# Linear attention levels with 64-row products: one query operation for both heads, results by head

## The chip, the cores and the metric

One core of a Trainium2 chip runs the whole program in one launch. The metric is device time in microseconds (us) of one execution, median of three. The engines are TensorE (PE), VectorE (DVE), ScalarE (ACT), GpSimd (POOL) and the DMA queues that SyncE (SP) starts.

## The reference, cut to what matters

The program is a two-layer block (pooling, gated linear attention, softmax attention, MLP) followed by a second block (Mamba-2, gated delta rule, MLP). The change touches the gated linear attention alone, 4 heads of 64, over 256 context and 512 latent tokens:

```python
def gla_chunk_scan(q, k, v, la, s0, strict):
    mask = np.tril(np.ones((C, C), bool), k=-1 if strict else 0)[:, :, None]
    def step(S, inp):
        qc, kc, vc, lc = inp
        b = jnp.cumsum(lc, axis=2)
        o_inter = jnp.einsum('bhid,bhde->bhie', qc * jnp.exp(b), S)
        diff = b[:, :, :, None, :] - b[:, :, None, :, :]
        decay = jnp.exp(jnp.where(mask, diff, -jnp.inf))
        A = jnp.einsum('bhid,bhjd,bhijd->bhij', qc, kc, decay)
        o = o_inter + jnp.einsum('bhij,bhje->bhie', A, vc)
```

It runs forward (f) and backward (b) in time. The decay is per channel d, so A is no plain product of queries and keys.

## The kernel before, in words

The function `gla` computes this in tiles of 128 tokens. It is called twice: for layer 0 (all C = 6 tiles, `first` = 0, nb = 6) and for layer 1 (the 4 latent tiles, `first` = 2, nb = 4). For stable exponents it splits each 128x128 matrix A into **levels**: at level m (1, 2, 4, ... 64) the queries are the second halves of blocks of 2m tokens and the keys the first halves, and both are scaled against the decay at the middle. 7 levels forward and 7 backward make 14 levels a layer. Only half of the tokens are queries in a level, so a tile has 64 query columns.

A level goes through four engines, each with its own written-out order and semaphores:

- POOL, lines 1142 to 1155: 4 subtractions give the exponents in `E` (two buffers, by `lev % 2`); it may begin level lev once `level_ready` of lev - 2 is up, then it raises `diff`.
- ACT, line 1106: one Exp over `E`, raises `ee`.
- DVE, `decayed(lev)`, lines 1206 to 1221: one product for the keys into `F` (L1216) and two products of 64 partitions each for the queries into `Q` (L1220), then `level_ready`. A partition group of 64 is one head of a pair. `Q` is zero outside: head 0's queries have data in partitions 0 to 63 and zeros below, head 1's the reverse; a MEMSET (L1162) sets the zeros at the start of the stage.
- PE, L1039: for each tile and pair of heads one fp32 product over all 128 rows, whose 128 moving columns are 64 queries of head 0 and 64 of head 1. The zeros keep the heads apart. 4 products fill a bank of PSUM and raise `a_full`; banks go round by 6, and PE waits for `a_read` before it fills one again. An fp32 product is two LDWEIGHTS and two MATMUL records in the trace.
- DVE, L1238: a COPY_PREDICATED per bank (512 columns) puts the wanted entries into `A`, raises `a_read`.

DVE's order is: `decayed(lev + 1)`, then the copies of level lev, and so on, so PE works on level lev + 1 while DVE copies level lev:

```python
                for lev in range(1, 2 * LEVELS + 1):
                    if lev < 2 * LEVELS:
                        decayed(lev + 1)
                    ...
                    for n in range(nb // 2):
                        done = (lev - 1) * (nb // 2) + n
                        dve.wait_ge(a_full, done + 2)
```

After the 14 levels ACT waits for the last `a_full`, and writes the state decays into the same memory `qd` that held `Q` (L1113); DVE multiplies them (L1244), and chunk states, output products (L1067, L1070) and the gate follow. Ahead of the levels the own-token products L1025 contract over 64 rows each: its banks alternate between partitions 0 to 63 and 64 to 127. The stage loads nothing large and has a barrier at both ends. PE also runs the pool mix (L1006) after levels 3 and 6, ACT its results (L1085).

## Time and profile before

| | |
|---|---|
| three runs | 4133.22, 4142.72, 4141.39 us, median 4141.39 |
| the profiled execution | 4152.68 us, span 4149.8 us |
| PE busy over the span | 3610.2 us, 87% |
| DVE busy | 2273.7 us, 55% |
| ACT, POOL busy | 1255.5 us, 30%; 1162.5 us, 28% |
| mean granted TensorE clock | 0.916 |
| levels of layer 0 | about 314.5 to 400 us of the span |
| levels of layer 1 | about 1560.5 to 1618 us |

Times are us from the span's start. PE is the matmul, PEld the weight load beside it; L12 is line 12. In a row of the timeline several alike instructions in a row are merged: start, how long they took together, engine, line, operation, tiles, count, and in brackets the idle time before and who ended it. A granted clock of 1.00 is 2.4 GHz, 0.50 is 1.2 GHz.

### The profile page before, as it was taken

The numbers are of one execution on the slowest core, as the hardware profiler recorded it, in microseconds if no ns is written. First come the engines' busy times: TensorE is split into PE (matmuls) and PEld (weight loads), VectorE is DVE, ScalarE is ACT, GpSimd is POOL, SyncE is SP. The second block draws the span as 40 slices with busy tenths as digits, with TensorE's granted clock in tenths as the row PEclk, the third lists the DMA queues.
The fourth block names the chain that finished last, engine by engine and source line by source line (L and its number), as shares of the span: only waits on it lengthen the run. The fifth ranks groups of instructions, "written<-read, shape, count | busy, mean of one in ns | idle before, by whom it ended". The sixth has DMA issues, their size and how long they took to land. (4 is left out here: it accounts for less than half of the span.)

```text
span 4149.8 us, 56879 instructions
## 1 busy us (share of the span) xinstructions
PE 3610.2 (87%) x22004; PEld 3014.9 (73%) x22004; DVE 2273.7 (55%) x3284; ACT 1255.5 (30%) x1878; POOL 1162.5 (28%) x564
## 2 busy tenths in 40 slices
PE   5976797899998976889996999798999996987998
PEld 3766576788887765667885788677777775765886
DVE  4669462655546448535445588733666655326334
ACT  4123222211222123223323354432333432323222
POOL 5214002222222203024441333143222220423442
PEclk8988599899999988999998999899999997998998
DMA  4420001223222430013331211121011110212221
GB/s 164 154 93 1 0 1 61 77 97 112 97 91 93 142 105 1 1 58 115 117 111 44 77 66 71 36 102 67 32 47 37 41 47 1 102 61 72 98 95 60
DMA packets 85332, 295.30 MB, mean 71 GB/s; under 512 B 13506, under 2 KB 14082, under 8 KB 84740
## 3 DMA queue, kind: packets, MB, share of 16 engines
q1 hardware_dynamic: 84836, 290.74, 19.8%
q8 instruction: 154, 2.52, 0.2%
q10 hardware_dynamic: 288, 1.60, 0.1%
q14 instruction: 54, 0.44, 0.0%
HBM read 290.21 MB, written 2.10 MB: 70 GB/s over the span
## 5 line engine op out<-in xcount | busy, mean ns | idle before, releaser
L221 POOL TENSOR_TENSOR mlp_slab_lo<-slab,mlp_slab_hi 128x1024 fp32r<-128x1024 f32 x192 | 477.1, 2488 | 889.2 <-ACT mlp_slab_hi L204 889.2
L119 PE MATMUL banks<-mlp_hid_hi,mlp_slab_hi 128*128 128x512 f32 (+1 forms) x1024 | 375.0, 366 | 8.9 <-DVE mlp_hid_lo L1798 8.9
L120 PE MATMUL banks<-mlp_hid_lo,mlp_slab_hi 128*128 128x512 f32 (+1 forms) x1024 | 372.7, 364 | 0.0
L121 PE MATMUL banks<-mlp_hid_hi,mlp_slab_lo 128*128 128x512 f32 (+1 forms) x1024 | 372.4, 364 | 0.0
L204 ACT ACTIVATE mlp_slab_hi<-slab 128x1024 fp32r<-128x1024 f32 x192 | 202.4, 1058 | 528.8 <-PE banks L121 400.9
L119 PE MATMUL banks<-hT_mlp_hi,mlp_slab_hi 128*128 128x512 f32 (+1 forms) x768 | 276.6, 360 | 15.5 <-issue 8.7
L1798 DVE TENSOR_TENSOR mlp_hid_lo<-mlp_sq,mlp_hid_hi 128x512 fp32r<-128x512 f32 (+1 forms) x96 | 216.4, 2254 | 117.9 <-ACT mlp_hid_hi L1756 117.5
L120 PE MATMUL banks<-hT_mlp_lo,mlp_slab_hi 128*128 128x512 f32 (+1 forms) x768 | 275.7, 359 | 0.0
L121 PE MATMUL banks<-hT_mlp_hi,mlp_slab_lo 128*128 128x512 f32 (+1 forms) x768 | 274.9, 358 | 0.0
L119 PEld LDWEIGHTS banks<-mlp_hid_hi,mlp_slab_hi 128*128 128x128 f32 x1024 | 194.2, 190 | 43.8 <-DVE mlp_hid_lo L1798 13.8
L121 PEld LDWEIGHTS banks<-mlp_hid_hi,mlp_slab_lo 128*128 128x128 f32 x1024 | 194.0, 189 | 30.3
L120 PEld LDWEIGHTS banks<-mlp_hid_lo,mlp_slab_hi 128*128 128x128 f32 x1024 | 194.1, 190 | 29.6
L221 POOL TENSOR_TENSOR ssm_slab_lo<-slab,ssm_slab_hi 128x1024 fp32r<-128x1024 f32 x48 | 124.0, 2591 | 303.2 <-ACT ssm_slab_hi L204 303.1
L221 POOL TENSOR_TENSOR out_slab_lo<-slab,out_slab_hi 128x1024 fp32r<-128x1024 f32 x24 | 58.9, 2466 | 520.5 <-ACT out_slab_hi L204 520.5
L1795 DVE TENSOR_TENSOR mlp_sq<-mlp_tmp 128x512 f32<-128x512 f32 (+1 forms) x96 | 96.8, 1008 | 196.5 <-ACT mlp_tmp L1751 196.5
L221 POOL TENSOR_TENSOR gdn_slab_lo<-slab,gdn_slab_hi 128x1024 fp32r<-128x1024 f32 x48 | 116.2, 2424 | 283.1 <-ACT gdn_slab_hi L204 283.1
L406 DVE SCALAR_TENSOR_TENSOR mlp_vec_acc<-mlp_vec_slab,c_act,mlp_vec_acc 128x512 f32<-128x512 f32 x192 | 187.6, 1032 | 4.5 <-DMA mlp_vec_slab<-in_s_vec_mlp_dram 4.5
L119 PEld LDWEIGHTS banks<-hT_mlp_hi,mlp_slab_hi 128*128 128x128 f32 x768 | 147.8, 192 | 39.2 <-issue 13.2
L1751 ACT ACTIVATE mlp_tmp<-banks 128x512 f32<-128x512 f32 (+1 forms) x96 | 64.3, 670 | 357.9 <-PE banks L121 347.8
L121 PEld LDWEIGHTS banks<-hT_mlp_hi,mlp_slab_lo 128*128 128x128 f32 x768 | 147.4, 192 | 21.3
L120 PEld LDWEIGHTS banks<-hT_mlp_lo,mlp_slab_hi 128*128 128x128 f32 x768 | 147.7, 192 | 20.6
L221 POOL TENSOR_TENSOR proj_slab_lo<-slab,proj_slab_hi 128x1024 fp32r<-128x1024 f32 x32 | 80.4, 2519 | 262.6 <-ACT proj_slab_hi L204 262.6
(532 smaller groups left out, 9330.4 us busy)
## 6 DMA issues: line engine op xcount, KB each, us to landing
slab<-in_s_mlp_dram SPq DMA_DIRECT2D x192, 512.0 KB, 3.5
proj_vec_slab<-in_s_vec_proj_dram SPq DMA_DIRECT2D x64, 512.0 KB, 3.7
mlp_vec_slab<-in_s_vec_mlp_dram SPq DMA_DIRECT2D x64, 512.0 KB, 3.5
slab<-in_s_ssm_dram SPq DMA_DIRECT2D x48, 512.0 KB, 3.5
slab<-in_s_gdn_dram SPq DMA_DIRECT2D x48, 512.0 KB, 3.5
slab<-in_s_in_dram SPq DMA_DIRECT2D x32, 512.0 KB, 4.6
slab<-in_s_out_dram SPq DMA_DIRECT2D x24, 512.0 KB, 4.2
slab<-in_s_merge_ssm_dram SPq DMA_DIRECT2D x24, 512.0 KB, 3.5
```

The costliest lines, as they stand in the source:

```text
L119: nc.tensor.matmul(out, lhs.hi, rhs.hi, start=start, stop=False)
L120: nc.tensor.matmul(out, lhs.hi, rhs.lo, start=False, stop=False)
L121: return nc.tensor.matmul(out, lhs.lo, rhs.hi, start=False, stop=stop)
L204: self.nc.scalar.activation(hi, self.raw[s][:], ACT.Copy).then_inc(self.rounded, 1)
L221: self.nc.gpsimd.tensor_tensor(pair.lo[:], self.raw[u % slots][:], pair.hi[:].bitcast(F32), ALU.subtract).then_inc(self.split, 1)
L406: last = nc.vector.scalar_tensor_tensor(out=acc, in0=x, scalar=w, in1=acc, op0=ALU.mult, op1=ALU.add)
L1751: nc.scalar.activation(tmp[:, u % 2, :], source(u), ACT.Relu).then_inc(rel, 1)
L1795: nc.vector.tensor_tensor(sq[:, u % 2, :], tmp[:, u % 2, :], tmp[:, u % 2, :], ALU.mult).then_inc(squared, 1)
L1798: nc.vector.tensor_tensor(hid.lo[:, u, :], sq[:, u % 2, :], hid.hi[:, u, :].bitcast(F32), ALU.subtract).then_inc(hid_ready, 1)
```

## The change

- `Q` is now [128, 2, 2, tile, 64]: no half for each head, no zeros. One DVE operation over 128 partitions makes the queries of both heads of a pair. The MEMSET of `qd` goes, and `cleared` is awaited at 3, not 4.
- PE computes each head apart: rows 0 to 63 of `F` and `Q` for head 0, rows 64 to 127 for head 1, one straight after the other, 64 moving columns each. That is twice as many products with half the columns.
- Results are laid out by head: a **part** is up to 4 tiles (layer 0: parts of 4 and 2 tiles, M = 2; layer 1: one part of 4, M = 1) and fills two banks, one for each head. `a_full` is raised once for a part. PE waits until both banks are read.
- DVE copies one bank of a part for each head: 512 columns for a part of 4 tiles, 256 for one of 2.

```diff
+    parts = [(t, min(4, C - t)) for t in range(first, C, 4)]
+    M = len(parts)
...
-        Q = qd[:].rearrange("p d n -> p (d n)").rearrange("p (b h a t f) -> p b h a t f", b=2, h=2, a=2, f=64)
+        Q = qd[:, 0:2, :].rearrange("p d n -> p (d n)").rearrange("p (b a t f) -> p b a t f", b=2, a=2, f=64)
...
+        def filled(lev, j, h):
+            return 2 * ((lev - 1) * M + j) + h
...
-                    for n in range(nb // 2):
-                        done = (lev - 1) * (nb // 2) + n
-                        if done >= 6:
-                            pe.wait_ge(a_read, done - 4)
-                        for e in range(4):
-                            ch = first + 2 * n + e // 2
-                            last = nc.tensor.matmul(c.ps[:, done % 6, e * P:(e + 1) * P].rearrange("p (h f) -> p h f", h=2),
-                                                    F[:, lev % 2, e % 2, ch * P:(ch + 1) * P], Q[:, lev % 2, :, e % 2, ch, :], start=True, stop=True)
+                    for j, (t0, count) in enumerate(parts):
+                        if filled(lev, j, 1) >= 6:
+                            pe.wait_ge(a_read, filled(lev, j, 1) - 4)
+                        for e in range(2 * count):
+                            ch = t0 + e // 2
+                            for h in range(2):
+                                r = slice(64 * h, 64 * h + 64)
+                                last = nc.tensor.matmul(c.ps[:, filled(lev, j, h) % 6, e * 64:(e + 1) * 64], F[r, lev % 2, e % 2, ch * P:(ch + 1) * P],
+                                                        Q[r, lev % 2, e % 2, ch, :], start=True, stop=True)
                         last.then_inc(a_full, 1)
...
-                nc.vector.memset(qd[:], 0.0).then_inc(cleared, 1)
...
-                        dve.wait_ge(a_full, (lev - 2) * (nb // 2) + 1)
+                        dve.wait_ge(a_full, (lev - 2) * M + 1)
                     nc.vector.tensor_tensor(F_[:, :, :, keys], k_[:, :, :, keys], E_[:, :, :, keys], ALU.mult)
-                    for h in range(2):
-                        r = slice(64 * h, 64 * h + 64)
-                        to = Q[r, lev % 2, h, :, first:, :].rearrange("p a t f -> p a (t f)").rearrange("p a (b m) -> p a b m", m=m)
-                        last = nc.vector.tensor_tensor(to, q_[r, :, :, queries], E_[r, :, :, queries], ALU.mult)
-                    last.then_inc(level_ready, 1)
+                    to = Q[:, lev % 2, :, first:, :].rearrange("p a t f -> p a (t f)").rearrange("p a (b m) -> p a b m", m=m)
+                    nc.vector.tensor_tensor(to, q_[:, :, :, queries], E_[:, :, :, queries], ALU.mult).then_inc(level_ready, 1)
...
-                    for n in range(nb // 2):
-                        done = (lev - 1) * (nb // 2) + n
-                        dve.wait_ge(a_full, done + 2)
...
-                        nc.vector.copy_predicated(second(A[:, first + 2 * n:first + 2 * n + 2].rearrange("p t a h f -> p (t a h) f")),
-                                                  mask.to_broadcast([P, 8, 64 // m, m]),
-                                                  c.ps[:, done % 6, :].rearrange("p (e b m) -> p e b m", e=8, m=m)).then_inc(a_read, 1)
+                    for j, (t0, count) in enumerate(parts):
+                        dve.wait_ge(a_full, (lev - 1) * M + j + 2)
+                        for h in range(2):
+                            n = filled(lev, j, h)
+                            if lev > 1:
+                                dve.wait_ge(a_read, n - 2 * M + 2)
+                            nc.vector.copy_predicated(second(A[:, t0:t0 + count, :, h].rearrange("p t a f -> p (t a) f")),
+                                                      mask.to_broadcast([P, 2 * count, 64 // m, m]),
+                                                      c.ps[:, n % 6, 0:128 * count].rearrange("p (e b m) -> p e b m", e=2 * count, m=m)).then_inc(a_read, 1)
```

How DVE's order reads in layer 0 before, from the keys of level 5 on (L1216 the keys, L1220 the queries, L1238 the copies):

```order
L1216 TENSOR_TENSOR gla_r<-gqk,gla_r 128x48x16
L1220 TENSOR_TENSOR gla_qd<-gqk,gla_r 64x768 x2
L1238 COPY_PREDICATED gla_A<-const,banks 128x64x8 x3
L1216 TENSOR_TENSOR gla_r<-gqk,gla_r 128x24x32
L1220 TENSOR_TENSOR gla_qd<-gqk,gla_r 64x768 x2
L1238 COPY_PREDICATED gla_A<-const,banks 128x32x16 x3
```

And with the change, at the same place:

```order
L1222 TENSOR_TENSOR gla_r<-gqk,gla_r 128x48x16
L1224 TENSOR_TENSOR gla_qd<-gqk,gla_r 128x768
L1242 COPY_PREDICATED gla_A<-const,banks 128x8x8x8 x2
L1242 COPY_PREDICATED gla_A<-const,banks 128x4x8x8 x2
L1222 TENSOR_TENSOR gla_r<-gqk,gla_r 128x24x32
L1224 TENSOR_TENSOR gla_qd<-gqk,gla_r 128x768
L1242 COPY_PREDICATED gla_A<-const,banks 128x8x4x16 x2
L1242 COPY_PREDICATED gla_A<-const,banks 128x4x4x16 x2
```

One of two query operations is gone from each level, and three copies have become four, two of them of half size. On PE, the level products of layer 0 before (36 are three levels of 12, L1006 is the pool mix):

```order
L1039 MATMUL banks<-gla_qd,gla_r 128x128 x36
L1006 MATMUL banks<-gla_m,gla_wp 128x512
L1006 MATMUL banks<-gla_m,gla_wp 128x256
L1039 MATMUL banks<-gla_qd,gla_r 128x128 x36
```

and with the change:

```order
L1046 MATMUL banks<-gla_qd,gla_r 128x64 x72
L1012 MATMUL banks<-gla_m,gla_wp 128x512
L1012 MATMUL banks<-gla_m,gla_wp 128x256
L1046 MATMUL banks<-gla_qd,gla_r 128x64 x72
```

Nothing has moved between them; each product of 128 columns has become two of 64.

## Rows read from the trace of the kernel before

**Rows 1.** The page, busy time of engines over the span.
```profile
PE 3610.2 (87%) x22004; PEld 3014.9 (73%) x22004; DVE 2273.7 (55%) x3284; ACT 1255.5 (30%) x1878; POOL 1162.5 (28%) x564
```
**Rows 2.** Busy time by window, levels of layer 0 and of layer 1; PEclk is the clock.
```profile
core 0: us, PE busy (x) PEld busy (x) DVE busy (x) ACT busy (x) POOL busy (x), PEclk, DMA share, GB/s
314.50:400.00 85.50, 55.10 (x344) 51.37 (x344) 82.77 (x86) 25.04 (x23) 47.42 (x48) 0.84 0.00 1
1560.50:1618.00 57.50, 38.24 (x249) 34.19 (x244) 56.12 (x71) 17.02 (x20) 34.88 (x48) 0.85 0.00 1
```
**Rows 3.** Timeline of one level of layer 0.
```profile
341.04 1.90 DVE L1238 COPY_PREDICATED gla_A<-const,banks 128x512 f32<-128x512 uint32 x3
...
341.06 4.58 PE L1039 MATMUL banks<-gla_qd,gla_r 128*128 128x128 f32 x24 [2.36 <-DVE gla_qd L1220]
341.08 0.83 POOL L1150 TENSOR_TENSOR gla_r<-gla_bT 128x384 f32<-128x384 f32 x1 [1.86 <-DVE gla_qd L1220]
...
342.84 1.47 DVE L1216 TENSOR_TENSOR gla_r<-gqk,gla_r 128x768 f32<-128x768 f32 x1
343.45 1.55 POOL L1151 TENSOR_TENSOR gla_r<-gla_bT 128x384 f32<-128x384 f32 x1
344.23 2.55 DVE L1220 TENSOR_TENSOR gla_qd<-gqk,gla_r 64x768 f32<-64x768 f32 x2
345.04 1.49 ACT L1106 ACTIVATE gla_r<-gla_r 128x1536 f32<-128x1536 f32 x1 [4.29 <-POOL gla_r L1151]
346.81 1.95 DVE L1238 COPY_PREDICATED gla_A<-const,banks 128x512 f32<-128x512 uint32 x3
```
**Rows 4.** Timeline of one level of layer 1.
```profile
1583.33 1.32 DVE L1238 COPY_PREDICATED gla_A<-const,banks 128x512 f32<-128x512 uint32 x2
...
1583.36 3.78 PE L1039 MATMUL banks<-gla_qd,gla_r 128*128 128x128 f32 x16 [1.62 <-DVE gla_qd L1220]
...
1585.61 1.79 DVE L1220 TENSOR_TENSOR gla_qd<-gqk,gla_r 64x512 f32<-64x512 f32 x2
1586.19 1.06 ACT L1106 ACTIVATE gla_r<-gla_r 128x1024 f32<-128x1024 f32 x1 [3.04 <-POOL gla_r L1154]
...
1587.43 0.73 DVE L1238 COPY_PREDICATED gla_A<-const,banks 128x512 f32<-128x512 uint32 x1
```
**Rows 5.** Line L1220 by itself, layers 0 and 1: ns min/median/max.
```profile
L1220 DVE TENSOR_TENSOR gla_qd<-gqk,gla_r x28: 923/956/1661, 315.4 to 392.1; 64x768 f32<-64x768 f32 x28
L1220 DVE TENSOR_TENSOR gla_qd<-gqk,gla_r x28: 673/690/1214, 1561.1 to 1614.9; 64x512 f32<-64x512 f32 x28
```
**Rows 6.** Line L1216, the keys, 128 partitions, layer 0.
```profile
L1216 DVE TENSOR_TENSOR gla_r<-gqk,gla_r x14: 947/1400/1747, 314.6 to 390.3; 128x768 f32<-128x768 f32 x14
```
**Rows 7.** Timeline, first levels of layer 0, then of layer 1.
```profile
318.26 3.25 DVE L1220 TENSOR_TENSOR gla_qd<-gqk,gla_r 64x768 f32<-64x768 f32 x2
...
321.55 3.63 DVE L1238 COPY_PREDICATED gla_A<-const,banks 128x512 f32<-128x512 uint32 x3
...
1563.12 0.69 DVE L1216 TENSOR_TENSOR gla_r<-gqk,gla_r 128x512 f32<-128x512 f32 x1 [0.62 <-ACT gla_r L1106]
```
**Rows 8.** Timeline, PE: a full-clock level; 64 columns; 64 rows; 64 by 64.
```profile
335.86 2.84 PE L1039 MATMUL banks<-gla_qd,gla_r 128*128 128x128 f32 x24
...
2356.02 3.68 PE L2052 MATMUL banks<-ssm_xdt,ssm_dec 128*128 128x64 f32 x32
...
1553.72 2.82 PE L1025 MATMUL banks<-gqk 64*128 64x128 f32 x32 [0.69 <-ACT gla_bT L1102]
...
2916.81 1.15 PE L2283 MATMUL banks<-gdn_own,gdn_am 64*64 64x64 f32 x32
```
**Rows 9.** Busy time by window, around the products of L2052.
```profile
2356.00:2380.00 24.00, 22.96 (x162) 21.37 (x161) 17.61 (x32) 9.06 (x17) 6.92 (x3) 1.00 0.12 45
```
**Rows 10.** Timeline, end of the levels of layer 1.
```profile
1615.64 2.05 PE L1039 MATMUL banks<-gla_qd,gla_r 128*128 128x128 f32 x16 [1.17 <-DVE gla_qd L1220]
1617.73 2.77 ACT L1113 ACTIVATE gla_qd<-gla_bT 128x3072 f32<-128x3072 f32 x1 [5.52 <-PE banks L1039]
```
**Rows 11.** Timeline, DVE at the start of the stage in layer 0.
```profile
267.07 2.62 DVE L1162 MEMSET gla_qd<- 128x3072 f32 x1 [0.59 <-issue]
...
283.25 0.53 DVE L1181 RECIPROCAL gla_qk_stat<-gla_qk_stat 128x60 f32<-128x60 f32 x1 [9.50 <-ACT gla_qk_stat L1094]
```

More of the change, by code:

```diff
@@ L1043, in _ @@
                         pool_mix(lev // 3 - 1)
-                pe.wait_ge(a_read, LEVELS * nb + 1)
+                pe.wait_ge(a_read, 4 * LEVELS * M + 1)
                 for t in range(C):
@@ L1110, in _ @@
                         pool_out(lev // 3 - 1)
-                act.wait_ge(a_full, LEVELS * nb + 1)
+                act.wait_ge(a_full, 2 * LEVELS * M + 1)
                 nc.scalar.activation(qd[:], bT[:], ACT.Exp).then_inc(decays, 1)
@@ L1214, in decayed @@
                     if lev > 2:
-                        dve.wait_ge(a_full, (lev - 2) * (nb // 2) + 1)
+                        dve.wait_ge(a_full, (lev - 2) * M + 1)
                     nc.vector.tensor_tensor(F_[:, :, :, keys], k_[:, :, :, keys], E_[:, :, :, keys], ALU.mult)
-                    for h in range(2):
-                        r = slice(64 * h, 64 * h + 64)
-                        to = Q[r, lev % 2, h, :, first:, :].rearrange("p a t f -> p a (t f)").rearrange("p a (b m) -> p a b m", m=m)
-                        last = nc.vector.tensor_tensor(to, q_[r, :, :, queries], E_[r, :, :, queries], ALU.mult)
-                    last.then_inc(level_ready, 1)
-                dve.wait_ge(cleared, 4)
+                    to = Q[:, lev % 2, :, first:, :].rearrange("p a t f -> p a (t f)").rearrange("p a (b m) -> p a b m", m=m)
+                    nc.vector.tensor_tensor(to, q_[:, :, :, queries], E_[:, :, :, queries], ALU.mult).then_inc(level_ready, 1)
+                dve.wait_ge(cleared, 3)
                 decayed(1)
@@ L1231, in _ @@
                     mask = second((c.mask_f if d == 0 else c.mask_b)[:, (lev - 1) % LEVELS:(lev - 1) % LEVELS + 1, :]).bitcast(U32)
-                    for n in range(nb // 2):
-                        done = (lev - 1) * (nb // 2) + n
-                        dve.wait_ge(a_full, done + 2)
-                        if lev > 1:
-                            dve.wait_ge(a_read, done - nb // 2 + 2)
-                        nc.vector.copy_predicated(second(A[:, first + 2 * n:first + 2 * n + 2].rearrange("p t a h f -> p (t a h) f")),
-                                                  mask.to_broadcast([P, 8, 64 // m, m]),
-                                                  c.ps[:, done % 6, :].rearrange("p (e b m) -> p e b m", e=8, m=m)).then_inc(a_read, 1)
-                dve.wait_ge(a_read, LEVELS * nb + 1)
+                    for j, (t0, count) in enumerate(parts):
[7 more added lines that the diff above has]
+                                                      c.ps[:, n % 6, 0:128 * count].rearrange("p (e b m) -> p e b m", e=2 * count, m=m)).then_inc(a_read, 1)
+                dve.wait_ge(a_read, 4 * LEVELS * M + 1)
                 dve.wait_ge(decays, 2)
```

## The prediction

> **What bounds the kernel now.** I read the page first. TensorE is busy for 87% of the span [rows 1], so one would look there. But the change touches only the level loops, two stretches of 85.5 and 57.5 us, and there the busy times by window say something else: VectorE is busy for 82.77 of 85.50 us and 56.12 of 57.50 us, TensorE for 55.10 and 38.24 [rows 2]. Then I read the timeline of one level. In layer 0 VectorE goes without a gap from three copies (341.04) to the keys (342.84), the two query operations (344.23) and the next copies (346.81): a level takes 5.77 us, all of it VectorE [rows 3]. TensorE stood idle for 2.36 us before its products, and the reason named is the query operation L1220. In layer 1 the same loop is 1583.33 to 1587.43, 4.10 us [rows 4]. So VectorE sets the pace of 28 levels, and what it sheds shortens the stage, as long as POOL, ACT and TensorE keep up. The stages behind have barriers between them and start earlier by as much.
>
> **The query operations.** Alone, one takes 0.956 us on 768 columns and 0.690 us on 512, over 64 partitions [rows 5]. What does one over 128 partitions cost? The keys are such an operation with the same 768 columns, and their shortest is 0.947 us [rows 6], so VectorE's time follows the columns and not the partitions. The merged operation costs what one of the two did. Which one goes? The pair takes 2.58 us from start to start of the next (344.23 to 346.81), more than 2 x 0.956, because the first runs beside POOL's last subtraction, which itself takes 1.55 us in place of 0.83 [rows 3]. With a gap of 0.03 us the second takes 0.99, the first 1.59. POOL's work stays, so its cost to VectorE stays, and the free one is what goes: 0.99 us a level in layer 0. In the second level both are stretched (318.26 to 321.55, 3.29 us [rows 7]), and 3.29 - 1.59 = 1.70 go. Layer 0: 13 x 0.99 + 1.70 = 14.5 us. In layer 1 it is 0.69 + 0.03 = 0.72 a level. In its first level nothing is won, since the next keys wait 0.62 us for ACT there already [rows 7]. Layer 1: 13 x 0.72 = 9.4 us.
>
> **The copies.** In layer 0 three copies of 512 columns (1.80 us, 0.60 each [rows 3]) become two of 512 and two of 256. From 768 to 512 columns a query operation loses 0.266 us [rows 5], so 256 columns cost 0.27 us, and a half copy 0.60 - 0.27 = 0.33. Together 1.86 to 1.87, 0.07 more a level, 1.0 us over 14. In layer 1 there are two copies of 512 before and after. The copies of the finest levels are slower (three in 321.55 to some 325 [rows 7]) and stay so, as they touch the same entries. The destination is now cut in more pieces for one instruction. No row shows that alone; the copies of different levels in [rows 3] and [rows 4] have different pieces at the same 0.60, so I take nothing, and 0.1 us a copy (84 copies, 8 us) as the far bound.
>
> **The MEMSET.** It takes 2.62 us, but VectorE then idles 9.50 us until ACT gives the roots [rows 11]. Nothing is won, in either layer. If that cover were gone it would be 2 x 2.6.
>
> **TensorE.** A product before is two records of 128 columns; a level of layer 0 has 24 of them and takes 2.84 us at full clock [rows 8], 4.58 us where the clock changes in between [rows 3]; 16 in layer 1 take 2.05 us at full clock [rows 10] and 3.78 us at low clock [rows 4]. After, there are 48 and 32, with 64 moving columns. Half the columns do not make them faster: 32 records of 128 rows with 64 moving columns take 3.68 us, (3.68 - 0.28) / 31 = 0.110 us each, the spacing of the 128-column ones ((2.84 - 0.28) / 23 = 0.111) [rows 8]. So one record costs a weight load of 128 columns. All hangs on whether the two row halves work at the same time. Two rows say so. The own products use halves of the rows in turns of 8 records and take 2.82 us for 32, 0.082 each, less than a lone load allows. The delta-rule products alternate between row halves at every product, as the change will, and need 1.15 us for 32, 0.030 each, though their loads have 64 columns, which by halving 0.110 would be 0.055 alone [rows 8]. They pair fully. I take full pairing: 48 records in 24 slots of 0.11, the same 2.84 us a level as before, 16 slots in layer 1. The far bound is no pairing, 0.110 a record.
>
> Does TensorE then come in time? VectorE's new level is 5.77 - 0.99 + 0.07 = 4.85 us. Copying now waits for a part of 16 slots (2.05 us, at low clock 3.78), where it waited for one bank; DVE comes for it 4.85 us after `level_ready`. Enough. The part of two tiles waits for the bank pair that DVE reads 1.2 us after `level_ready`, while the first part is still running, so nothing is lost. In layer 1 the new level is 3.38 us, and the single part at low clock is ready after 3.78: a wait of 0.4. The granted clock there is 0.85 over the loop [rows 2], so about 30% of 14 levels, 4 levels or so, wait, and it costs at most 1.7 us; I take 1.0. After the last level ACT waits for TensorE's last result: 1615.64 to 1617.73 [rows 10], the same slots as now.
>
> **POOL and ACT.** From `level_ready` to the end of ACT's Exp two levels ahead it is 341.04 to 346.53, 5.49 us [rows 3]; the keys that need it come 4.85 + 1.87 = 6.72 us after. In layer 1 it is 1583.33 to 1587.25, 3.92 [rows 4], against 3.38 + 1.22 = 4.60. They have 1.2 and 0.7 us to spare.
>
> **The sum**: 14.5 + 9.4 - 1.0 - 1.0 = 21.9 us. Against the profiled execution 4152.7 gives 4130.8 us. That execution lies 11.3 us above the median of the three; against the median, 4141.4 - 21.9 = 4119.5 us. The three runs spread over 9.5 us, 0.23%, so about 0.3% (12.4 us) is what a measurement can tell from no change. My bound for faster is 4129.0.
>
> **Rivals.**
> *Row halves do not pair in full, at full clock.* At 0.110 a record TensorE needs 5.3 us a level in layer 0 and 3.5 in layer 1 and becomes the bound. The gain is 14 x 0.49 + 13 x 0.58 = 14.4 us, less what the last level adds to the way to ACT (24 and 16 slots of 0.11, 4.4 us): 4131.4, no change. A row speaks for full clock: where TensorE is busy for 22.96 of 24 us with products that include the 64-column ones, it is granted 1.00 [rows 9]. The pairing rows speak against it. The Trainium skill, "TensorE: Matmul & The Clock Gate", section on LDWEIGHTS, gives a rule that speaks for this rival: a weight load takes a time set by its columns and not by its rows, so a load of 64 rows is no cheaper, and the loads are doubled here; by that alone TensorE's time would double. The Trainium skill, "TensorEngine Tiling (Array Packing)", section Key Properties, has the counter-rule, that different tiles load and multiply in parallel; the trace agrees with it (0.082 and 0.030 us against 0.110 [rows 8]).
> *Slower: no pairing, and the clock as granted now.* With 0.84 and 0.85 [rows 2] a record costs 0.131 us; a level of layer 0 is 6.29 us on TensorE against 5.77 now, of layer 1 4.19 against 4.10. That is 7.3 + 1.2 us, and 5.2 on the way to ACT behind the last levels: 4155 us. It decides as soon as records come further apart than 5.77 / 48 = 0.120 us in layer 0. Held at low clock (15 spacings in 3.36 us, 0.224 a record [rows 4]) it would be 10.8 and 7.2 us a level, above 4240.
> *Pairing holds, but the clock is lower than now.* Each half of the rows now streams columns half the time. If all levels ran at low clock, layer 0 would take 24 x 0.224 = 5.4 us a level and layer 1 3.8: gains of 5 and 4 us, and 4 lost behind the last levels, some 4136. More low levels than now, but not all, gives 4124 to 4132.
> *The merged operation costs double*, VectorE being charged by partition: then 4142. [Rows 6] speak against it.
>
> **How the numbers follow.** The forecast has 0.70 (its own range 4110 to 4127, from the runs' spread and 0.1 us a copy); pairing with a lower clock, or pairing in part only, 0.14, about half of it on either side of 4129; no pairing at full clock 0.05; slower 0.07; other causes of no change 0.04. Faster 0.77, same 0.16, slower 0.07. The range of 4108 to 4133 us leaves out the slower cases and the far ends.
>
> **What would show it.** In the profile after: query operations x14 a layer at medians near those of the keys, 1.4 to 1.6 us in layer 0; levels of about 4.85 and 3.4 us from first copy to first copy; half copies near 0.33 us apart; level products of 48 records in about 2.9 us at full clock; the loops at 71 and 48 us. Wrong would be: VectorE waiting for PE before copies in most levels, records 0.11 us apart without partners, VectorE waiting for ACT before the keys, or a granted clock in the loops well under 0.84.

## The result: 4105.3 us, 36 us faster, with a lower clock in the loops than forecast

The changed kernel takes 4105.26 us (median of 8 runs, 4088.94 to 4121.81), the kernel before 4141.16 us in the runs beside it (8 runs, 4133.22 to 4152.71): ratio 0.9913, 95% interval 0.9888 to 0.9939. Faster was forecast, at 4119.5 us in a range from 4108 to 4133. The gain came out at 36 us in place of 22, and the time 3 us below the lower end of the range. The profiled execution took 4095.27 us, its span is 4093.5 us.

The page of the kernel after, busy time and instruction queue:

```profile
PE 3608.2 (88%) x22564; PEld 3025.4 (74%) x22564; DVE 2231.0 (55%) x3268; ACT 1253.4 (31%) x1878; POOL 1159.5 (28%) x564
...
q8 instruction: 141, 2.31, 0.2%
```

Against [rows 1] VectorE shed 42.7 us, and TensorE got 560 records more with no more busy time. The busy times of the two level loops, from the first keys to the first product with the decays, answer to [rows 2]:

```profile
core 0: us, PE busy (x) PEld busy (x) DVE busy (x) ACT busy (x) POOL busy (x), PEclk, DMA share, GB/s
308.90:386.30 77.40, 70.22 (x680) 65.82 (x680) 63.63 (x86) 24.38 (x20) 44.42 (x48) 0.59 0.01 1
1505.50:1563.70 58.20, 51.70 (x461) 47.08 (x459) 42.95 (x58) 19.23 (x21) 32.90 (x48) 0.57 0.01 1
```

The same two stretches of the kernel before, between the same two instructions (the windows of [rows 2] begin and end elsewhere):

```profile
314.60:399.00 84.40, 55.10 (x344) 51.37 (x344) 81.67 (x86) 23.94 (x19) 47.42 (x48) 0.84 0.00 1
1560.50:1620.60 60.10, 38.24 (x249) 34.19 (x244) 56.59 (x72) 19.62 (x21) 34.88 (x48) 0.86 0.00 1
```

So the loops gave 7.0 and 1.9 us, 9 in all. VectorE's work fell by more than forecast, 18.0 us (81.67 to 63.63) and 13.6 (56.59 to 42.95) for 13.5 and 9.4. But the granted clock fell from 0.84 and 0.86 to 0.59 and 0.57, TensorE is busy for 70.22 of 77.40 us where it was for 55.10 of 84.40, and where VectorE waits for it, in six of layer 0's 14 levels and ten of layer 1's, it sets the pace now. What VectorE waited for is told by the lines of the stretch 308 to 388 us, layer 0's loop:

```profile
line engine op names shapes xcount | busy us, mean ns | idle before us <-releasers
L1242 DVE COPY_PREDICATED gla_A<-const,banks 128x512 f32<-128x512 uint32 x28 | 22.9, 884 | 9.2 <-PE banks L1046 9.2
...
L1224 DVE TENSOR_TENSOR gla_qd<-gqk,gla_r 128x768 f32<-128x768 f32 x14 | 16.4, 1172 | 0.0
...
L1242 DVE COPY_PREDICATED gla_A<-const,banks 128x256 f32<-128x256 uint32 x28 | 13.0, 529 | 1.9 <-PE banks L1046 1.9
```

The copies waited 9.2 + 1.9 = 11.1 us for TensorE; in layer 1's loop it is 13.1.

L1046 holds the level products now, L1242 the copies, L1224 the queries, L1222 the keys. In the timeline a level at low clock stands like this (its counterpart is [rows 3]):

```profile
start us, us, engine line op out<-in xcount [idle before <-releaser]
336.74 1.32 DVE L1242 COPY_PREDICATED gla_A<-const,banks 128x512 f32<-128x512 uint32 x2 [0.93 <-PE banks L1046]
...
338.44 0.77 DVE L1242 COPY_PREDICATED gla_A<-const,banks 128x256 f32<-128x256 uint32 x2 [0.39 <-PE banks L1046]
...
339.11 0.95 DVE L1222 TENSOR_TENSOR gla_r<-gqk,gla_r 128x768 f32<-128x768 f32 x1
339.98 0.95 DVE L1224 TENSOR_TENSOR gla_qd<-gqk,gla_r 128x768 f32<-128x768 f32 x1
...
341.86 1.36 DVE L1242 COPY_PREDICATED gla_A<-const,banks 128x512 f32<-128x512 uint32 x2 [0.92 <-PE banks L1046]
```

From copies to copies it is 5.12 us (336.74 to 341.86), of which VectorE waits 0.93 + 0.39 for TensorE. The keys and the queries take 0.95 us each here and not some 1.5: while VectorE waits, POOL's subtractions get done, so that its operations no longer run beside them. That is why its busy time fell by more than forecast. Where TensorE's results are there in time, later in the same loop, a level is what was forecast: 367.30 - 362.47 = 4.83 us, without a wait.

```profile
362.47 1.94 DVE L1242 COPY_PREDICATED gla_A<-const,banks 128x512 f32<-128x512 uint32 x4
...
364.32 1.55 DVE L1222 TENSOR_TENSOR gla_r<-gqk,gla_r 128x768 f32<-128x768 f32 x1
...
365.80 1.57 DVE L1224 TENSOR_TENSOR gla_qd<-gqk,gla_r 128x768 f32<-128x768 f32 x1
...
367.30 1.96 DVE L1242 COPY_PREDICATED gla_A<-const,banks 128x512 f32<-128x512 uint32 x4
```

TensorE's own rows show that the halves of the rows pair at either clock: at full clock 32 records take 2.00 us, 16 slots with (2.00 - 0.28) / 15 = 0.115 us between them; at low clock, granted 0.50, TensorE is busy without a break and does 101 records in 11 us, 0.218 for two. The first two rows are the timeline's, the last is the busy time by window.

```profile
352.29 2.00 PE L1046 MATMUL banks<-gla_qd,gla_r 64*128 64x64 f32 x32 [0.25 <-DVE gla_qd L1224]
...
357.44 25.90 PE L1046 MATMUL banks<-gla_qd,gla_r 64*128 64x64 f32 x240 [1.68 <-DVE gla_qd L1224]
...
333.00:344.00 11.00, 11.00 (x101) 10.82 (x100) 8.10 (x14) 2.97 (x2) 6.64 (x9) 0.50 0.01 1
```

So where do 36 us come from, when the loops give 9? I cut both traces at the barriers between stages. The busy times by window of five stages before (linear attention, attention and multilayer perceptron of layer 0, linear attention and attention of layer 1):

```profile
265.49:448.34 182.85, 113.64 (x724) 102.12 (x724) 148.32 (x190) 65.81 (x86) 55.60 (x56) 0.77 0.04 11
451.85:628.40 176.55, 171.74 (x868) 124.83 (x868) 97.76 (x244) 47.50 (x109) 0.00 (x0) 0.82 0.00 1
716.83:1319.82 602.99, 573.31 (x3280) 505.18 (x3280) 343.44 (x376) 131.99 (x162) 166.43 (x64) 0.96 0.27 98
1513.74:1663.73 149.99, 91.58 (x572) 79.98 (x572) 118.75 (x174) 58.76 (x84) 40.84 (x56) 0.76 0.04 13
1667.53:1797.48 129.95, 124.14 (x740) 93.51 (x740) 76.37 (x164) 38.36 (x77) 0.00 (x0) 0.95 0.00 1
```

and the same five after:

```profile
259.71:435.90 176.19, 129.92 (x1060) 117.69 (x1060) 127.79 (x189) 65.92 (x86) 52.37 (x56) 0.65 0.04 12
439.41:589.57 150.16, 145.34 (x868) 107.97 (x868) 95.33 (x244) 47.43 (x109) 0.00 (x0) 0.98 0.00 1
679.34:1265.67 586.33, 567.94 (x3280) 501.65 (x3280) 343.65 (x376) 131.80 (x162) 167.87 (x64) 0.97 0.28 101
1458.76:1607.02 148.26, 104.81 (x796) 92.64 (x796) 102.62 (x159) 58.73 (x84) 39.55 (x56) 0.65 0.04 14
1610.83:1740.88 130.05, 124.30 (x740) 93.71 (x740) 76.39 (x164) 38.33 (x77) 0.00 (x0) 0.95 0.00 1
```

The two stages that the edit changes gave 6.7 and 1.7 us. Layer 0's attention, whose instructions did not change (868 records of TensorE in both), went from 176.55 to 150.16 us with the granted clock from 0.82 to 0.98, and the perceptron behind it, with the same 3280 records, from 602.99 to 586.33. These two give 43.1 of the 56.3 us between the two spans; the projection ahead of the change, which the edit does not touch either and which takes 187 to 192 us in profiles of either kernel, gives 5 more. Between the medians it is less, since the profiled execution of before lies 11.5 us above its median and that of after 10.0 us below.

### The profile page after: what moved, and what is told of

The parts are those of the page before. It is cut to its first block and busy times, and to the rows that moved or that the text cites. A ratio compares the mean times of both kernels' runs of the same rounds, so it can differ in the third digit from the quotient of the medians.

```text
span 4093.5 us, 57957 instructions
## 1 busy us (share of the span) xinstructions
PE 3608.2 (88%) x22564; PEld 3025.4 (74%) x22564; DVE 2231.0 (55%) x3268; ACT 1253.4 (31%) x1878; POOL 1159.5 (28%) x564
## 5 line engine op out<-in xcount | busy, mean ns | idle before, releaser
L119 PEld LDWEIGHTS banks<-mlp_hid_hi,mlp_slab_hi 128*128 128x128 f32 x1024 | 194.4, 190 | 43.3 <-DVE mlp_hid_lo L1802 13.5
```

The source lines that it names most:

```text
L119: nc.tensor.matmul(out, lhs.hi, rhs.hi, start=start, stop=False)
```

## The experiments

My theory for the loops: the clock fell because TensorE streams 64 columns in a slot where it streamed 128, though the slots take the same time. Its rival: the clock fell because VectorE's faster levels bring the products closer together or at other moments. For the two foreign stages the question was whether they vary from run to run, or with something that the change moves.

**Products that stream their columns twice.** The kernel with the change, every product (but the last of a part) over its 64 columns twice in a row; the second copy falls on the entry that the next product writes, so the results are the same.

```diff
-last = nc.tensor.matmul(c.ps[:, filled(lev, j, h) % 6, e * 64:(e + 1) * 64], F[...], Q[r, lev % 2, e % 2, ch, :], ...)
+w = 2 if e < 2 * count - 1 else 1
+last = nc.tensor.matmul(c.ps[:, filled(lev, j, h) % 6, e * 64:(e + w) * 64].rearrange("p (w f) -> p w f", w=w), F[...],
+                        Q[r, lev % 2, e % 2, ch, :].unsqueeze(1).to_broadcast([64, w, 64]), ...)
```

> The changed kernel, but each level product streams its 64 query columns twice (128 moving columns; the second copy lands in the bank's next 64 columns and is overwritten by the next product). Same weight loads, same slots of 0.11 us, same results. Theory 1, the granted clock in the level loops fell from 0.84 to 0.59 because each record streams only 64 columns: now the clock is back at 0.8 or more, VectorE no longer waits 24 us for TensorE before its copies (under 8 us), and the two loops, first keys to the first product with the decays, take about 71 and 50 us in place of 77.4 and 58.2. Theory 2, the clock fell for another reason (row halves used in turns, or shorter levels): clock near 0.6, waits near 24 us, loops 77 and 58. Attention of layer 0: 150 us if it is the levels' ending that decides how it begins, whatever the columns.

Measured: 4105.25 us (8 runs, 4098.41 to 4109.23), ratio to before 0.9933 (0.9912 to 0.9954). Busy time of the two loops by window:

```profile
314.90:385.70 70.80, 50.13 (x680) 46.45 (x680) 67.64 (x85) 23.98 (x19) 48.06 (x48) 0.90 0.01 2
1528.20:1578.90 50.70, 35.55 (x461) 32.07 (x459) 45.44 (x58) 19.06 (x21) 35.41 (x48) 0.90 0.01 2
```

With the same 680 records the clock is back at 0.90, TensorE is busy for 50.13 us in place of 70.22, and the loops take 70.8 and 50.7 us: twice the columns, and 14 us less. The copies wait 0.9 us for TensorE in layer 0 and 2.4 in layer 1, in place of 11.1 and 13.1. One level of layer 0 in the timeline:

```profile
336.14 1.96 DVE L1243 COPY_PREDICATED gla_A<-const,banks 128x512 f32<-128x512 uint32 x4
336.28 2.90 PE L1047 MATMUL banks<-gla_qd,gla_r 64*128 64x128 f32 x48 [1.95 <-DVE gla_qd L1225]
...
340.96 2.00 DVE L1243 COPY_PREDICATED gla_A<-const,banks 128x512 f32<-128x512 uint32 x4
```

48 records in 2.90 us, the slots of [rows 8], and 4.82 us a level. That the whole kernel was no faster than the change lies in layer 0's attention: it takes 171.7 us here, in place of 150.2, so the 150 of the expectation did not come, though the levels end as in the change.

**Both kernels looked at once more.** Neither is edited.

> The kernel before, unchanged, profiled again. In the two profiles attention of layer 0 took 176.6 us before and 150.2 after, the MLP of layer 0 603.0 and 586.4, the projection of layer 0 192.3 and 187.2. Theory A, these belong to the kernels: here again 177 and 603. Theory B, they differ from execution to execution: attention anywhere from 150 to 180, MLP anywhere from 586 to 603.

> The changed kernel, unchanged, profiled again. Theory A: attention of layer 0 again 150 us, MLP again 586, clock in the levels again near 0.59, loops 77.4 and 58.2. Theory B: attention and MLP take other values, up to 177 and 603.

Measured, one run each: before 4137.28 us, its attention 171.8 and its perceptron 597.9 us; the change 4108.4 us, 150.3 and 586.6 us. The loops of before are again 84.4 and 60.2 us, those of the change 79.0 and 59.6. Neither kernel repeats its durations exactly (attention of before was 176.6, its perceptron 603.0), but the two foreign stages are part of the difference in both pairs.

**Half of the query work alone.** The kernel before with head 0's queries only; it leaves out head 1's decayed queries, so head 1's half of the columns holds the zeros of the MEMSET.

```diff
-                    for h in range(2):
+                    for h in range(1):
```

> The kernel before, with VectorE making the queries of head 0 alone in each level (head 1's product is left out, its half of the operand stays zero); TensorE does the 128-column products over 128 rows as before. It has the VectorE side of the change without its TensorE side. Theory 1 (64 columns lower the clock): VectorE sheds 0.99 and 0.72 us a level, the clock stays near 0.84, and the loops take 84.4 - 14 = 70 and 60.1 - 10 = 50 us. Theory 2 (shorter levels lower the clock): clock under 0.7 and loops of 75 and 56 or more.

Measured: 4121.14 us (10 runs, 4098.2 to 4129.61), ratio 0.9954 (0.9930 to 0.9978), loops of 74.0 and 52.4 us. VectorE makes one query operation a level here, as in the change, and TensorE still streams 128 columns a record. The two loops by window:

```profile
310.60:384.60 74.00, 49.30 (x344) 45.98 (x344) 69.62 (x71) 23.95 (x20) 57.58 (x48) 0.91 0.00 1
1539.80:1592.20 52.40, 33.84 (x249) 29.45 (x244) 45.62 (x57) 19.31 (x21) 41.23 (x48) 0.97 0.00 1
```

The clock is 0.91 and 0.97. Shorter levels do not lower it; the rival falls. Layer 0's loop is 3.2 us longer than in the experiment before, and 4 us longer than expected: VectorE is busy for 2.0 us more (69.62 for 67.64), and its keys wait for ACT in four levels, 1.8 us in all, as here:

```profile
334.70 1.63 DVE L1216 TENSOR_TENSOR gla_r<-gqk,gla_r 128x768 f32<-128x768 f32 x1 [0.43 <-ACT gla_r L1106]
```

**Layer 0's attention, moved in time.** First idea: the stage is short or long by the moment at which it begins relative to the clock's changes. A MEMSET on VectorE, of a buffer that nobody reads, ahead of the stage shifts it: in the change by 470, 1400 and 2650 columns (0.4, 1.2 and 2.2 us), in the kernel before by 3530 (some 3 us), in the wide one by 1730 (some 1.5 us).

```diff
+        idle = sb("idle", [P, 470])
...
+                if l == 0:
+                    nc.vector.memset(idle[:], 0.0)
```

> The changed kernel with one VectorE MEMSET of 470 columns (about 0.45 us) ahead of the attention of layer 0. In six profiles the clock rises to full 5.9 to 6.7 us after attention's start. Where that was 5.9 to 6.1 us (before twice, the wide kernel, the one-query kernel) it fell again at 12.7 to 13 us and stayed low for 48 to 58 us, and attention took 172 to 177 us; where it was 6.3 and 6.7 us (the change twice) it did not fall, and attention took 150. Theory moment (it is decided by where attention's start lies against the moments at which the clock is set, which the program does not move): starting 0.45 us later, the rise comes 0.45 us sooner after the start, the low stretch comes back, attention takes about 172 us and the whole 20 to 25 us more than the change. Theory content (what the changed levels do to TensorE decides it): attention stays at 150, the whole within 2 us of the change.

> The kernel before with a MEMSET of 3530 columns (about 3.0 us) ahead of the attention of layer 0. Theory moment: the start moves past to where the rise is again over 6.2 us after it; attention loses its low stretch, takes about 150 + 3 us, and the whole kernel is about 19 us faster than before although it does 3 us more work. Theory content: attention takes 172 to 177 + 3 us, the whole 3 us slower than before.

> The wide kernel (each level product streams its 64 columns twice) with a MEMSET of 1730 columns (about 1.5 us) ahead of the attention of layer 0. Theory moment: the rise comes about 4.4 us after attention's start, where no run has been yet; if only 5.9 to 6.1 is the bad moment, attention takes 150 + 1.5 us and the whole is about 20 us under the wide kernel, near 4085 us. Theory content: 172 + 1.5 us, the whole 1.5 us over the wide kernel.

> The change with a VectorE memset of 1400 columns (about 1.2 us) ahead of layer 0's attention. If the moment at which the stage begins decides its clock, then some shift should turn the change's fast attention slow: time 4122 to 4128 and attention 170 or more. If the change's attention is fast for another reason, such as what TensorE did in the stage ahead, it stays at 150 us and the time at about 4102 (4095 to 4110).

> As the one with 1.2 us, with 2650 columns (about 2.2 us). The moment decides: 4123 to 4129 at one of the shifts tried (0.4, 1.2, 2.2 us). Another reason: 4103 (4096 to 4111), attention 150.

Measured: the change with the three delays 4101.34 us (4 runs, ratio 0.9919, 0.9892 to 0.9946), 4097.6 (4 runs, 0.9904, 0.9878 to 0.993) and 4099.65 (4 runs, 4092.58 to 4116.79, 0.9921, 0.9891 to 0.9951); attention took 150.2, 152.0 and 153.2 us in their profiles, the MEMSET included. No shift made it long there; one unprofiled run, at 4116.79 us, may have had the long duration. The kernel before with its delay: 4141.67 us (10 runs, ratio 1.0014, 0.9999 to 1.003), with two of the ten at 4128, of which the profiled one has attention at 153.8 us. The wide kernel with its delay: 4078.41 us (4 runs, 0.9885, 0.984 to 0.993), three of them at 4076 to 4079 and one at 4106.87, where the undelayed one had all eight at 4098 to 4109. So the stage has two durations, some 150 and some 172 us, within one and the same kernel. In the wide kernel a shift changed how often each comes, in the other two it hardly did; a rule by which the moment alone decides is not borne out.

**The place of the perceptron's code.** TensorE in the kernel before stops at the start of the perceptron's later passes and waits for nothing:

```profile
1028.71 0.79 PE L119 MATMUL banks<-hT_mlp_hi,mlp_slab_hi 128*128 128x512 f32 x1 [4.48 <-issue]
```

Its lines, over that stage, of before:

```profile
L119 PE MATMUL banks<-hT_mlp_hi,mlp_slab_hi 128*128 128x256 f32 (+1 forms) x512 | 176.2, 344 | 12.4 <-issue 8.7 <-DVE hT_mlp_lo L618 3.7
```

and of after:

```profile
L119 PE MATMUL banks<-hT_mlp_hi,mlp_slab_hi 128*128 128x256 f32 (+1 forms) x512 | 173.9, 340 | 3.7 <-DVE hT_mlp_lo L618 3.7
```

8.7 us of issue are gone, and the instruction queue's packets fell from 154 to 141. The change puts 336 more products, with a load each, into layer 0's loop (344 records before, 680 after), ahead of that code. If it is the place of the code that counts, other instructions ahead of it do the same: the kernel before with 320 waits that are already met, at the end of TensorE's part in the linear attention of layer 0 (that stage took 184.4 us, 1.5 more).

```diff
                 pe.wait_ge(a_read, LEVELS * nb + 1)
+                if l == 0:
+                    for _ in range(320):
+                        pe.wait_ge(a_read, LEVELS * nb + 1)
```

> The kernel before with 160 instructions more in TensorE's program, all waits that are long fulfilled, at the end of the linear attention stage of layer 0, where TensorE idles for 17 us. The change has 672 instructions more ahead of the MLP loop (160 more modulo 256). In the profiles of before, before again and one-query, TensorE stands still for 3.3 to 4.7 us at the start of the second and third pass of that MLP, with nothing that it waits for, instruction fetches (queue 8) go on through all passes (155 packets in all), and the stage takes 598 to 603 us; in those of the change, twice, and wide there is no such stop, fetches end in the second pass (141 packets), and it takes 586 to 592. Theory placement (the stops belong to where the loop lies in TensorE's program): here 141 to 145 packets, no stops, MLP of layer 0 about 586 us, the whole about 10 us under before. Theory chance or something else in the change: 598 to 603 us and 155 packets.

Measured: 4127.55 us (10 runs, 4106.23 to 4139.82), ratio 0.9965 (0.9942 to 0.9988). The stage takes 587.03 us, and the queue has 137 packets:

```profile
706.68:1293.71 587.03, 567.11 (x3280) 500.68 (x3280) 341.50 (x376) 131.81 (x162) 167.62 (x64) 0.98 0.28 100
...
q8 instruction: 137, 2.24, 0.2%
```

The first row is the busy time by window, the second is from the page. Two of the 320 waits make one instruction: TensorE has 753 semaphore instructions here and 593 before, the 160 of the expectation. Over all profiles the stage splits cleanly. Five of kernels without the padding or the change (before twice, its delayed and its filled form, half the query work) have 154 or 155 packets, one or two stops of 3.1 to 4.6 us, and 597 to 604 us; the eleven others have 137 or 141 packets, no such stop, and 585 to 591. It is not the time that the waits take: before with the 3 us MEMSET keeps its 155 packets, a stop of 4.25 us and 598 us. The place of the code does it.

How much it is worth can't be read from the two medians, 14 us apart, since attention's two durations are mixed in either. Of the ten padded runs four lie at 4106.23 to 4116.02 us, five at 4132.87 to 4139.82, and the profiled one, with a long attention of 170 us, at 4122.23; of the nineteen of before beside them one lies at 4121.62, two at 4131, sixteen at 4136.67 to 4145.33. Between the upper groups it is 8.7 us (medians 4133.5 and 4142.2). The waits cost something themselves: from the last work of linear attention to the first of attention it is 7.5 us with them (in both padded profiles) and 4.2 without. So the place alone is worth some 12 us of the whole, by estimate.

**Attention with TensorE's pauses filled.** In the kernel before TensorE pauses twice as the first units of attention start, for 0.86 and 1.30 us, and some 2 us later the granted clock falls: its products take 0.70 and then 1.22 us for two, and for 57.9 us it is busy without a break at 0.50 (last row, busy time by window):

```profile
460.38 0.70 PE L1386 MATMUL banks<-attn_qkT 64*128 64x256 f32 x4 [0.86 <-ACT attn_qkT L1332]
462.37 0.44 PE L1407 MATMUL banks<-const,attn_p 128*128 128x128 f32 x2 [1.30 <-ACT attn_p L1340]
462.74 0.70 PE L1386 MATMUL banks<-attn_qkT 64*128 64x256 f32 x2
...
466.50 1.22 PE L1386 MATMUL banks<-attn_qkT 64*128 64x256 f32 x2
...
464.60:522.50 57.90, 57.90 (x174) 38.59 (x173) 26.64 (x86) 11.45 (x36) 0.00 (x0) 0.50 0.00 1
```

The change has the same pauses at the same place, 0.80 and 1.29 us, and in its two profiles and those with the delays the clock does not fall behind them: the pauses alone do not decide.

I filled the pauses with ten products of the identity into a part of a bank that nobody reads, in the kernel before and in the wide one.

```diff
+                if l == 0:
+                    pe.wait_ge(placed, 9)
+                    for _ in range(4):
+                        nc.tensor.matmul(c.ps[:, 7, 384:512], c.ident, c.ident, start=True, stop=True)
                 pe.wait_ge(placed, 2 * C + 1)
...
+                    if l == 0 and n == 0:
+                        for _ in range(6):
+                            nc.tensor.matmul(c.ps[:, 7, 384:512], c.ident, c.ident, start=True, stop=True)
                     pe.wait_ge(exped, n + 2)
```

> The kernel before, with ten products of the identity (128 columns each, into a part of a bank that nobody reads) put into TensorE's two pauses at the start of layer 0's attention: four where it waits 0.86 us for the transposed queries, six where it waits 1.30 us for the first exponentials. Nothing else changes. Theory D (the pauses at the first context units are what lets the clock fall 12 to 13 us into the stage): the stage takes 150 us instead of 170 to 177, the granted clock stays at full level in it, and the time is about 4119 (4114 to 4124), in every run, with no second value near 4140. Theory E (the level is decided by something else, such as the phase in which the stage begins): the stage stays at 170 to 177 us in most runs and the time at 4135 to 4143. If the filling moves the code of the multilayer perceptron behind it to a better place, up to 14 us more come off: seen in that stage's own duration.

> The change with its products streaming twice, and the same ten products in the two pauses of layer 0's attention. Theory D: attention takes 150 us in each run and the time is 4080 (4074 to 4086) without a second value near 4105. Theory E: it stays near 4105 (attention 172) in most runs.

Measured: before, filled, 4121.46 us (10 runs, 4118.21 to 4125.72), ratio 0.9964 (0.9947 to 0.9982). The runs of the unfilled kernel beside it fall into two groups, five at 4117.35 to 4123.92 us with a granted clock of 0.922 to 0.924 over the run, and ten at 4139.64 to 4146.27 with 0.917 to 0.919; the filled one has no time in the upper group, 0.921 to 0.924 in each run. Wide, filled: 4078.94 us (5 runs, 4075.21 to 4081.57), ratio 0.9855 (0.9832 to 0.9877). TensorE's timeline in the filled kernel before, where the pauses were:

```profile
455.47 1.06 PE L1380 MATMUL banks<-const 128*128 128x128 f32 x8
456.46 0.70 PE L1390 MATMUL banks<-attn_qkT 64*128 64x256 f32 x4
457.09 1.60 PE L1408 MATMUL banks<-const 128*128 128x128 f32 x12
...
463.17 0.70 PE L1390 MATMUL banks<-attn_qkT 64*128 64x256 f32 x2
```

and the stage by window:

```profile
447.88:597.90 150.02, 147.37 (x888) 110.17 (x888) 95.35 (x244) 47.38 (x109) 0.00 (x0) 0.98 0.00 1
```

TensorE does more work and the stage is 26 us shorter than in the profile of before. With the pauses open the clock may fall behind them, with the pauses filled none of 15 runs has a time of the upper group. That it is the pauses and not merely ten products more was not tested: the same ten elsewhere in the stage would tell. Wide and filled is the fastest version I found, steadily ahead of both kernels.

**The sum of the parts.** The kernel before with both the waits and the filling, and the change with the filling.

> The kernel before with both foreign parts taken away: the 320 waits that are already met (they move the code of the multilayer perceptron) and the ten products. If the parts add up: 4141 less 13.5 (placement) less 20 (attention) = 4107 (4103 to 4112), one value, the perceptron at 586 to 588 us and attention at 150; the change with the same filling is then 7 to 10 us below it, which is what its loops gain. If they overlap, or something else is in the 36 us, it is at 4115 or more.

> The change with the ten products in the two pauses of layer 0's attention. If attention's two durations are the whole of the spread of the change's runs (4089 to 4122), its slow runs go: every run between 4089 and 4110, median 4100 (4096 to 4104). If something else spreads them, values near 4120 stay.

Measured: before, padded and filled, 4111.05 us (12 runs, 4104.27 to 4113.61, ratio 0.9952, 0.9934 to 0.9969), the change, filled, 4093.02 us (5 runs: 4082.18, 4082.58, 4093.02, 4094.14, 4100.06; ratio 0.9912, 0.9877 to 0.9946). The kernel before beside them has sixteen runs at 4111.20 to 4146.57 us, median 4132.7 (a seventeenth, at 8653.22 us, is left out). The first came 4 us above its expectation's middle and holds one group of values; the second came 7 us below its own, lost its values near 4120 but kept a spread of 18 us. Their difference is 18 us, and not the 7 to 10 I had written. Some 3 us of it are the waits, which the change does not have. Much of the rest is in the loops of the profiled run of the change, filled, a run that lies 10 us below its own median:

```profile
310.90:385.80 74.90, 67.52 (x680) 63.58 (x680) 67.62 (x86) 24.15 (x19) 47.27 (x48) 0.61 0.00 1
1503.30:1556.90 53.60, 44.55 (x461) 40.39 (x458) 45.20 (x58) 18.95 (x21) 34.11 (x48) 0.68 0.01 2
```

74.9 and 53.6 us here, 77.4 and 58.2 in the change's profile. How much of each loop is granted low clock varies from run to run, and so does the loops' gain: 9.0 us in one profile, 16.0 in another (84.4 + 60.1 less 74.9 + 53.6), 5.9 in a third (79.0 and 59.6), and between these in the three delayed ones. Layer 1's attention adds to it: some 126 us in this profile and in four others with the change's edit (the three wide ones and the longest delay), 130 in all the rest.

## Why the prediction was too small

- **VectorE's side held.** A merged query operation took 0.95 us alone and 1.55 to 1.57 beside POOL, as the keys do; VectorE shed 18.0 and 13.6 us in the two loops (14.0 and 11.2 in the wide kernel, where it hardly waits), for 13.5 and 9.4 forecast; levels that do not wait took 4.83 us for 4.85 forecast. The rival of an operation that costs double is out.
- **The pairing held.** 48 records in the slots of 24, at 0.115 us a slot at full clock and 0.218 at low clock. By the load rule of the Trainium skill, "TensorE: Matmul & The Clock Gate", section on LDWEIGHTS, alone, TensorE's time would have doubled at the same clock, by estimate. The Trainium skill, "TensorEngine Tiling (Array Packing)", section Key Properties, has separate tiles load and multiply in parallel; the trace agrees with the second (two records in 0.115 us).
- **The step that failed inside the stage** is the clock: I priced low-clock waits at 1.0 us in layer 1, with the granted clock of [rows 2] carried over, and at nothing in layer 0 ("Enough."), though 24 slots at my own low-clock spacing of 0.224 us are 5.4 us, more than VectorE's level of 4.85. The clock fell to 0.59 and 0.57, the waits ahead of the copies rose to 11.1 us in layer 0 and 13.1 in layer 1, 24.2 in place of 1.0, and the loops gave 9.0 us for 22; 8.7 us came back because VectorE shed 31.6 us for the 22.9 forecast. The rival "pairing holds, but the clock is lower than now" had this mechanism and its place; its price was near too, with levels of 5.4 us for the measured 5.12. That it goes with the streamed columns is shown: with 128 in place of 64, and nothing else changed, the clock came back to 0.90, and the loops of 70.8 and 50.7 us are within 3 us of the 71 and 48 that were forecast. [Rows 9] misled me: of the 162 records in that window only 32 stream 64 columns, 3.7 us of 22.96 by their lines; the others stream 256 or 512, so its granted clock of 1.00 said nothing of a loop made of such products.
- **The step that failed in the sum** is one sentence: "The stages behind have barriers between them and start earlier by as much." They start earlier, but two of them also ran differently. In a chain of kernels: filling attention's pauses takes 4140.8 to 4121.5 us (19.3), placing the perceptron's code 4121.5 to 4111.1 (10.4), the change in place of the padding 4111.1 to 4093.0 (18.0), and taking the filling away gives back 12.2, to 4105.3. By construction this adds up to the 36 us; what it shows is rough sizes, since only the first and the third step compare kernels on the same chip (on the chip of the third, before is 4132.7), and since the padding's waits cost some 3 us, which the second step hides and the third counts for the change. So of the 36 us some 15 to 18 come with the change itself, and as much from places that the prediction named nowhere. Two errors of opposite sign made the total look nearer than it was: 13 us too much in the loops (22 for 9, by the profile) and 27 us unseen outside them (36 less 9).
- **Right for the sign, for half of the right reason.** Without the foreign parts the gain would have been some 15 to 18 us (4093.0 against 4111.1, with or without the 3 us of the waits). That this is near 22 is partly luck: it holds more waiting than forecast, more shed by VectorE than forecast, and loops that gave anything from 5.9 to 16.0 us.

What stays open: why the change by itself has its attention at the short duration in most runs, by their times, the wide kernel never in eight, and before in none of 8, 3 of 17, 1 of 19, 5 of 15 and 6 of 16. That the fall no longer comes with the pauses filled is shown; what decides in a single run is not. Nor is it shown why low clock takes more of a loop in one run than in another.

## What to carry to other kernels

Cut a trace at its barriers and compare every stage, also those that the edit does not touch: here they held half of the gain, and a padding of empty waits or ten useless products were worth some 9 and 19 us by themselves. When products are split over the row halves, the number of slots tells only half; look at how many columns each streams, since here TensorE, busy without a break at a granted 0.50, needed 5.12 us a level, and with twice the columns at a granted 0.90 it came in time for VectorE's 4.82. And a stage with two durations must be made steady (here by filling the pauses) before a change of 0.5% is read from medians: the padding's 14 us between medians are 9 between runs of the same group.

## What the runs showed of the hardware

- Products of 64 rows in pairs, behind loads of 128 columns: with 64 moving columns a granted clock of 0.59 in the loop, with 128 columns 0.90, at the same 680 records. TensorE was busy in all of 333 to 344 us and was granted 0.50 there, the lower of its two levels (1.2 of 2.4 GHz).
- Behind two pauses of some 0.9 and 1.3 us at the start of a stage the clock was low for 44 to 58 us in five profiles, 19 to 26 us of stage time, and stayed full in seven others with pauses of 0.7 to 0.9 and 1.3 us; ten products in the pauses (2.7 us of TensorE) went with the short duration in all four profiles, and none of the 32 runs of these four kernels has a time of the upper group.
- The place of a long loop's code in TensorE's program was worth 6 to 18 us of some 600 (597 to 604 against 585 to 591), with stops of up to 4.6 us that no semaphore explains, and 154 or 155 packets of the instruction queue where the better places had 137 and 141.
